# The value projection of a linear-attention block: values with tokens on the partitions, against values computed in weight units and turned by TensorE

## What is computed

```
h  = modulate(rmsnorm(x, g_mix), sh1, sc1)        # 512 tokens x 1024
hc = modulate(rmsnorm(ctx, g_mix), sh1c, sc1c)    # 256 tokens x 1024
z  = h @ w_in;  zc = hc @ w_in
q, k, v, g, dd, cb, cc, ch, ga, gb = split(z)     # q, k: 512 columns; v: 1024 columns
heads = 4; q, k per head: 128 columns; v per head: 256 columns
kv[chunk] = (k * exp(b_last - b)).T @ v           # v is needed with tokens first
```

## Time and profile before

| what | value |
|---|---|
| median of 3 runs | 2156.66 us (2156.39 to 2161.26) |
| the profiled execution | 2161.26 us, span of its instructions 2159.5 us |
| TensorE matmul busy | 2138.0 us, 99% of the span |
| VectorE, ScalarE, GpSimd busy | 949.3, 877.7, 906.1 us |
| granted TensorE clock, mean | 0.994 |

### The profile page before, as it was taken

One profiled execution on the slowest core, in us unless ns is written; L12 is line 12 of the kernel. 1 busy time (PEld: TensorE's weight loads), 2 busy tenths in 40 slices (PEclk: granted clock), 3 DMA queues, 4 the chain that ended last, 5 costly groups with the idle time before them and its releaser, 6 DMA issues.

```text
span 2159.5 us, 29386 instructions
## 1 busy us (share of the span) xinstructions
PE 2138.0 (99%) x10741; PEld 1755.8 (81%) x10741; DVE 949.3 (44%) x1392; ACT 877.7 (41%) x1325; POOL 906.1 (42%) x463
## 2 busy tenths in 40 slices
PE   8999999999999999999999999999999999999997
PEld 6888888888888888888878888888888888888886
DVE  3206555643364222124974333222788874333211
ACT  3415555743243222234564322223666753333222
POOL 3322333344435444454854444443333334444442
PEclk8999999999999999999999999999999999999999
DMA  8221222166533222333122222233222212222231
GB/s 307 69 68 59 79 78 69 55 220 211 174 139 107 97 97 83 88 99 114 41 98 97 97 97 92 80 93 104 79 79 78 68 61 98 96 97 95 80 97 68
DMA packets 63809, 216.41 MB, mean 100 GB/s; under 512 B 7104, under 2 KB 8256, under 8 KB 62592
## 3 DMA queue, kind: packets, MB, share of 16 engines
q1 hardware_dynamic: 63744, 215.55, 30.2%
HBM read 213.42 MB, written 2.10 MB: 100 GB/s over the span
## 4 chain that ended last, share of the span: by engine, by line
PE 92%; DVE 3%; ACT 2%; issue 1%; DMA 1%; SPq 0%; DVEq 0%; ACTq 0%
PE ps L552 27%; PE ps L554 27%; PE ps L553 27%; PE ps L783 1%; PE ps L784 1%; PE ps L782 1%; PE ps L877 1%; PE ps L1125 1%; PE ps L887 1%; DMA ada_w<-in_w_ada_first 1%; DVE acc L2070 1%; DMA x_res<-in_x 1%; PE ps L630 0%; PE ps L1039 0%; PE ps L1037 0%
## 5 line engine op out<-in xcount | busy, mean ns | idle before, releaser
L399 POOL TENSOR_TENSOR w_lo<-w_raw,w_hi 128x1024 fp32r<-128x1024 f32 (+2 forms) x376 | 843.9, 2253 | 1149.7 <-ACT w_hi L1259 1148.9
L552 PE MATMUL ps<-h_hi,w_lo 128*128 128x512 f32 x1824 | 726.1, 398 | 1.5 <-DVE h_lo L1780 1.2
L554 PE MATMUL ps<-h_hi,w_hi 128*128 128x512 f32 x1824 | 711.4, 390 | 0.0
L553 PE MATMUL ps<-h_lo,w_hi 128*128 128x512 f32 x1824 | 711.3, 390 | 0.0
L1259 ACT ACTIVATE w_hi<-w_raw 128x1024 fp32r<-128x1024 f32 (+2 forms) x376 | 370.7, 995 | 597.3 <-PE ps L554 525.5
L552 PEld LDWEIGHTS ps<-h_hi,w_lo 128*128 128x128 f32 x1824 | 342.9, 188 | 81.4 <-issue 8.1
L554 PEld LDWEIGHTS ps<-h_hi,w_hi 128*128 128x128 f32 x1824 | 343.0, 188 | 72.7
L553 PEld LDWEIGHTS ps<-h_lo,w_hi 128*128 128x128 f32 x1824 | 343.2, 188 | 70.2 <-issue 1.0
L552 PE MATMUL ps<-gu_hi,w_lo 128*128 128x512 f32 x528 | 205.4, 389 | 0.0
L553 PE MATMUL ps<-gu_lo,w_hi 128*128 128x512 f32 x528 | 205.4, 389 | 0.0
L554 PE MATMUL ps<-gu_hi,w_hi 128*128 128x512 f32 x528 | 205.4, 389 | 0.0
(11 more groups left out here) (411 smaller groups left out, 2521.3 us busy)
## 6 DMA issues: line engine op xcount, KB each, us to landing
w_raw<-in_w_ffn_in SPq DMA_DIRECT2D x132, 512.0 KB, 3.4
w_raw<-in_w_hg SPq DMA_DIRECT2D x40, 512.0 KB, 3.4
w_raw<-in_w_ffn_out SPq DMA_DIRECT2D x48, 384.0 KB, 3.1
w_raw<-in_w_conv_gate SPq DMA_DIRECT2D x32, 512.0 KB, 3.5
w_raw<-in_w_merge SPq DMA_DIRECT2D x32, 512.0 KB, 4.6
ada_w<-in_w_ada SPq DMA_DIRECT2D x32, 512.0 KB, 4.5
w_raw<-in_w_ffn_out SPq DMA_DIRECT2D x48, 320.0 KB, 2.9
w_raw<-in_w_cp SPq DMA_DIRECT2D x20, 512.0 KB, 3.6
```

Source lines behind the costliest of these rows:

```text
L399: pool.tensor_tensor(w_lo[s][:, 0:n], raw[s][:, 0:n], w_hi[s][:, 0:n].bitcast(F32), ALU.subtract).then_inc(lo_done[s], 1)
L552: pe.matmul(out, wl, hi, start=first, stop=False)
L553: pe.matmul(out, wh, lo, start=False, stop=False)
L554: return pe.matmul(out, wh, hi, start=False, stop=last)
```

## The change

The value projection is written as eight more units, `u` = 8 to 15, of the form that the keys have: weights stationary, 24 matmuls of 512 columns and 24 of 256 each, with features on the partitions. ACT copies the first part and DVE the second into one of two buffers `vT`. For each unit `m` = `u - 8`, TensorE then turns the six tiles of 128 tokens with transposes (`pe_v_turn`) into a bank and a half of PSUM, and DVE copies them into `v_sb` with two copies. Turn `m` comes one unit late: after `context(m + 9)` for `m` = 0 to 5, between `lat(15)` and `context(15)` for `m` = 6, and inside `pe_gla` behind the first decay matmuls for `m` = 7. `values`, `bank_free` and `V_BANKS` go. The weights of rounds 2 and 3 are laid out as units on the host; each load has the size it had. `act_gla` waits at its start for all eight values, before its first Abs, where it waited for them ahead of the first `v_h` copy.

```
-V_BANKS = [4, 5, 6, 7, 0, 2], [1, 3, 6, 7, 4, 5]
+V_CTX_BANK = [6, 7, 6, 7, 6, 7, 6, 2]
...
+        vT = [at(f"vT{i}", [P, TC], F32, 82 + 3 * i) for i in range(2)]
...
+        def pe_v_turn(pe, m):
+
+            pe.wait_ge(S["qkv_lat_read"], m + 10)
+            pe.wait_ge(S["qkv_ctx_read"], m + 6)
+            if m >= 2:
+                pe.wait_ge(S["v_read"], m - 1)
+            for c in range(TTC):
+                bank = 4 + m % 2 if c < TT else V_CTX_BANK[m]
+                mm = pe.transpose(ps[:, bank, (c % TT) * P:(c % TT + 1) * P], vT[m % 2][:, c * P:(c + 1) * P], ident[:, :])
+            mm.then_inc(S["v_turned"], 1)
...
-            for u in (6, 7):
+            for u in range(6, 16):
                 lat(u)
+                if u == 15:
+                    pe_v_turn(pe, 6)
                 context(u)
...
-            for q in (2, 3):
-                for s in range(4):
-                    pe.wait_ge(lo_done[s], q + 1)
-                    for m in range(TTC):
-                        if s == 0:
-                            bank_free(q, m)
-                        mm = values(q, s, m)
-                        if s == 3 and m < TTC - 1:
-                            mm.then_inc(S["v_tokens"], 1)
-                    mm.then_inc(unit_done[s], 1)
+                if 8 < u < 15:
+                    pe_v_turn(pe, u - 9)
 
         def pe_gla(pe):
-            pe.wait_ge(S["v_read"], 10)
+            pe.wait_ge(S["v_read"], 7)
...
+                    if isinstance(h, int) and w == 0:
+                        pe_v_turn(pe, 7)
                     pe_unit(pe, 0, 0, q, h1_hi, h1_lo)
...
                     if isinstance(h, int) and w == 0:
-                        pe.wait_ge(S["v_read"], 2 * TTC)
+                        pe.wait_ge(S["v_read"], 8)
...
+                else:
+                    if u >= 10:
+                        act.wait_ge(S["v_turned"], u - 9)
+                    act.activation(vT[u % 2][:, 0:T], ps[:, u % 2, :], ACT.Copy).then_inc(S["qkv_lat_read"], 1)
...
         def act_gla(act):
+            act.wait_ge(S["v_read"], 8)
...
-                        if isinstance(h, int) and h == 0:
-                            act.wait_ge(S["v_read"], 2 * TTC)
...
         def dve_qkv(dve):
-            for u in range(4, 8):
+            def v_read(m):
+                dve.wait_ge(S["v_turned"], m + 1)
+                i = m % 2
+                out = v_sb[:, m // 2, :].rearrange("p (c v) -> p c v", v=HEAD_V)[:, :, i * P:(i + 1) * P]
+                dve.tensor_copy(out[:, 0:TT, :], ps[:, 4 + i, :].rearrange("p (c v) -> p c v", v=P))
+                dve.tensor_copy(out[:, TT:TTC, :], ps[:, V_CTX_BANK[m], 0:CTX].rearrange("p (c v) -> p c v", v=P))\
+                   .then_inc(S["v_read"], 1)
+
+            for u in range(4, 16):
                 s, q = u % 4, u // 4
+                if u == 15:
+                    v_read(6)
                 dve.wait_ge(unit_done[s], q + 1)
-                dve.tensor_copy(k_sb[:, s, T:TC], ps[:, 2 + u % 2, 0:CTX]).then_inc(S["qkv_ctx_read"], 1)
+                if u >= 10:
+                    dve.wait_ge(S["v_turned"], u - 9)
+                dve.tensor_copy(k_sb[:, s, T:TC] if u < 8 else vT[u % 2][:, T:TC], ps[:, 2 + u % 2, 0:CTX])\
+                   .then_inc(S["qkv_ctx_read"], 1)
...
-            for q in (2, 3):
-                for m in range(TTC):
...
+                if 8 < u < 15:
+                    v_read(u - 9)
+            v_read(7)
...
-    value_tiles = w_in[:, vv:g].reshape(4, 2, P, 2, 512).transpose(3, 0, 2, 1, 4).reshape(2, 4, P, D)
-    out["w_qkv"] = np.concatenate([units(w_in[:, q:vv]).reshape(2, 4, P, D), value_tiles])
+    out["w_qkv"] = units(w_in[:, q:g]).reshape(4, 4, P, D)
```

## The result

The changed kernel takes 2168.74 us (median of 5 runs, 2165.26 to 2171.16) against 2156.66 us (5 runs, 2155.09 to 2161.26): ratio 1.0052, 95% interval 1.0036 to 1.0068, so slower by 7.8 to 14.7 us. The prediction had the direction (slower) and a range up to 2167.0; the median is 1.7 us above it and 5.2 us above the predicted value. The profiled execution took 2170.59 us, with a span of 2168.9 us and a mean granted clock of 0.994.

What follows compares the result with a forecast made beforehand. The prediction took TensorE, busy 99% of the span, to bound the kernel. Projections +1.41 and transposes +5.33 gave +6.7 us, with other terms 0: 2156.66 + 6.7 = 2163.4 us (likeliest value 2163.5), range 2160.5 to 2167.

Steps and rivals of the forecast that it cites:

- Part 1, the projections: Value stage: eight units at 8.34 us, 66.72 us, replace 288 matmuls of 65.31 us: +1.41 us.
- Part 2, the transposes: Value stage: 48 f32 transposes at 0.110 us, 0.666 us per run of six, eight runs: +5.33 us.
- Part 3, hand-overs: Turns waiting for the copies of the unit before: covered, turn 7 closest (0.93 against 0.8 us); cost 0, 0.2 kept.
- Part 4, ACT's wait: ACT's earlier wait delays the first head's decay chain; 2.3 of 3.3 us cover remain at L854: cost 0.
- The sum: Whole kernel: +1.41 + 5.33 = +6.7 us, bounds +6.1 to +8.3, every stage behind starting that much later.
- Hand-overs stall: Turns wait 0.3 us each, or the first head's chain comes 2 to 3 us late: +9, 2165.9 us; chance 8%.
- The clock falls: Value stage: a unit with its turn at 1.2 instead of 2.4 GHz adds 9 us: 2172 us; chance 1%.
- Shared stationary: Value units: a repeated stationary block lets the third matmul run under the second: -15.5, 2141 us; chance 1%.

Runs made afterwards that it cites:

- Both experiments on their number: The changed kernel with twelve transposes a turn instead of six, 2171.52 us, and with two a turn, 2161.26 us.
- wait_late: The changed kernel with ACT's wait for the last value moved back to ahead of the first `v_h` copy: 2167.43 us, ratio 1.0049.
- second pair of profiles: Both kernels run and profiled once more, unchanged: before 2156.32 us (ratio 0.9995), after 2168.54 us (ratio 1.0047).

## Why the prediction missed

*Part 1, the projections: right.* Units at 8.34 (`u` = 9) and 8.35 us (`u` = 8), no faster for their shared stationary block.

*Part 2, the transposes: right.* 0.66 us a run, no entry cost behind a matmul of 256 columns, clock at 1.00. Both experiments on their number agree to 0.002 us a transpose. The rate of 81 ns that the Trainium skill gives for matmuls of 128 moving columns ("TensorE: Matmul & The Clock Gate", section "Back-to-back issue gap") would have made +5.3 as an estimate; the trace measured 108 to 110 ns and the stage +6.71.

*Part 3, hand-overs: right.* No wait ahead of any turn, also none ahead of turn 7, whose margin was called 0.1 us.

*Part 4, ACT's wait: right.* Margin at L830 (L854 before) 2.4 us against 2.3 predicted; *wait_late* gained nothing in the stage.

*The sum: right for the stage* (+6.71 measured, +6.7 predicted), *and the step behind it failed.* The prediction wrote: "All of it is TensorE time in a stage without idle, and every stage behind it starts that much later." The second half is the failed step: a shift of everything by the same amount was taken for granted. 465 us behind the stage stands a place where TensorE waits, 0.35 us in one profile of the kernel before and 1.2 us in the next, for a chain that begins with a DMA of 11.1 to 11.9 us. There the stages did not simply start 6.7 us later. The load took 1.5 us longer, the step grew by 1.46, and TensorE then ran for 3.4 us (6.8 us in the other profile) at half of its clock, which cost 1.4 (3.0) us. In the second pair of profiles the step grew by 0.8. The wait and the clock behind it are thus 2.9 and 3.8 us on top of 6.7; the medians put the excess at 4.9 to 5.4, and of that 4.7 went when the load was split. What is left in these profiles is the stall near 1585 us (0.8) and, in the second pair, the clock behind the later idle (1.6), which can fall on either kernel. The sum had no term for any of this: it put a later wait at nothing without a reason. The page of the kernel before gave a sign of it: its chain held 1% of DMA beside TensorE's 92%, the same chain by line named the load of `x_res` and the sum `acc` with 1% each, and I read only to 420 us.

*The rivals.* "Hand-overs stall" (+9, which on 2156.66 is 2165.7 and not the 2165.9 written) came nearest by its time, with a mechanism that did not occur. "The clock falls" was priced as an effect of transposes in their own stage. The clock there did not fall, with six or with twelve a turn. The Trainium skill's sentence that transposes don't count as busy for the clock in the same way (same page, "Part 4: PE-mode transpose") is neither borne out nor refuted by runs of six to twelve between units of 8 us. The clock fell at another place, behind a wait and eight matmuls of one column. "Shared stationary" did not occur.

*The chances.* Slower had 61%, and it was slower. The range was too narrow because every entry in it came from the stage itself; nothing stood for what a later wait could do.

*What stays open.* Why the load lands later in the changed kernel, and whether the instruction packet delays it; why *wait_late*, with a step of 2.18, shows no lower clock in its profile; what the stall of 0.65 us is; and whether every kernel with work added ahead of the load has a small excess.

No version beats the kernel before: with the load in four pieces it has 2156.59 us against 2156.91, inside the interval. In the changed kernel the split is worth 4.7 us and leaves it 7 us behind.

## What to carry to other kernels

A cost on the engine that bounds the kernel is added in full, but that is only the first term: list the places behind the change where that engine waits at all, however little, and what each wait begins with. Where it begins with a long DMA, a landing that comes a microsecond or so later can cost five, since the clock may fall behind the wait. A load whose consumer takes it block by block should be issued in blocks: here that removed the wait, at no cost that could be measured, and made the effect of the change the size that its own stage shows.

## What the runs showed of the hardware

A wait of 1.8 to 2.1 us of TensorE at the norm, in an otherwise full stream and with eight matmuls of one column behind it, was followed in three profiles of four by 3.4 to 6.8 us at half clock; waits of 0.35 to 1.5 us at the same place were not, in seven profiles. An idle of 1.65 us at another place, the same in all fourteen profiles, was followed within a microsecond by 3.4 us at half clock in nine of them and not in the other five. So one and the same wait can cost the clock in one execution and not in the next.

A matmul of f32 operands with a full 128x128 stationary block and two moving columns is two records of 0.112 us at the full clock, 0.22 us together, as much as a matmul of the units with 512 columns (0.227). 2.3 us into 16 of them, and 4.3 us into 40, the clock fell to the lower level, for 6.8 and 13.7 us.

An f32 transpose of 128x128 costs 0.108 to 0.112 us in runs of 2, 4, 6, 8 and 12, with nothing for the run's entry or exit, behind matmuls of 256 and of 512 columns.
